# Ten slots for the experts' rows and one kept query block, in place of nine and two

## What is computed

```python
h = rmsnorm(x); proj = h @ w_in        # conv branch, stick-breaking attention, S5 scan
x = x + concat(rmsnorm(parts)) @ w_out
x = x + memory_cross_attention(rmsnorm(x), rmsnorm(mem), w_mq, w_mkv, w_mo)
x = x + peer_ffn(rmsnorm(x), peer_wq, sub_keys, peer_u, peer_v)
```

## Time and profile before

| | |
|---|---|
| median of 3 runs | 1698.66 us (1697.45 to 1699.12) |
| the profiled execution | 1698.56 us, its span in the profile 1696.6 us |
| granted TensorE clock, mean | 0.989 |
| busy share of the span | PE 91%, DVE 69%, ACT 43%, POOL 34% |
| moved by DMA | 675.15 MB, 398 GB/s over the span |
| of it gathers (queue 0) | 536.90 MB |
| of it loads by SP (queue 1) | 137.00 MB |
| first gather issued at | 175.0 us |

### The profile page before, as it was taken

The page is one execution under the profiler, slowest core; times in us unless marked ns, Lnnn a source line. Parts: engine busy times, 40 slices in busy tenths (PEclk is TensorE's granted clock), DMA queues, the critical chain, the costliest instruction groups (busy, mean ns, idle before and its releaser), DMA issues.

```text
span 1696.6 us, 19718 instructions
## 1 busy us (share of the span) xinstructions
PE 1543.3 (91%) x6548; PEld 932.7 (55%) x6548; DVE 1177.5 (69%) x3053; ACT 735.4 (43%) x1971; POOL 577.2 (34%) x527
## 2 busy tenths in 40 slices
PE   9999899899999999888989889988999999777776
PEld 8877776346567776534645446534756554322232
DVE  7821899975877658986555667995656667666654
ACT  4142534763464323385433353465444334333333
POOL 0000344443334323343333343342333544333331
PEclk9999999999999999999999999999999999999999
DMA  9655999999999999999999999999999999999996
GB/s 390 251 199 223 373 416 421 420 421 420 421 420 421 421 419 421 416 417 421 421 421 415 421 414 421 386 422 407 421 412 418 421 421 422 421 421 421 422 420 260
DMA packets 93860, 675.15 MB, mean 398 GB/s; under 512 B 10408, under 2 KB 10688, under 8 KB 12224
## 3 DMA queue, kind: packets, MB, share of 16 engines
q0 software_dynamic: 73728, 536.90, 76.4%
q1 hardware_dynamic: 20032, 137.00, 19.9%
HBM read 672.81 MB, written 1.05 MB: 397 GB/s over the span
## 4 chain that ended last, share of the span: by engine, by line
PE 39%; DMA 32%; DVE 9%; ACT 4%; issue 2%; POOL 0%; DVEq 0%; ACTq 0%; POOLq 0%
DMA slots<-expert_rows,expert 32%; PE bank L967 22%; PE bank L465 8%; DVE slots L1967 5%; PE bank L656 3%; PE bank L952 2%; PE bank L955 2%; ACT diag L1467 1%; ACT coef L1485 1%; DVE sg L1512 1%; PE bank L744 1%; DVE htok L1789 1%; PE bank L723 1%; DVE x L1512 0%; ACT gel L1480 0%
## 5 line engine op out<-in xcount | busy, mean ns | idle before, releaser
L967 PE MATMUL bank<-slots,diag 128*128 128x512 f32 x1916 | 905.6, 609 | 126.8 <-ACT diag L1467 120.4
L1095 POOL DMA_INDIRECT slots<-expert_rows,expert x512 | 575.3, 1124 | 1094.6 <-PE bank L967 880.7
L1967 DVE CUSTOM_DVE_ANT_0 slots<-slots,htok 128x1024 f32<-128x1024 f32 x512 | 626.2, 1224 | 389.6 <-DMA slots<-expert_rows,expert 388.6
L967 PEld LDWEIGHTS bank<-slots,diag 128*128 128x128 f32 x1916 | 348.4, 193 | 537.5 <-issue 317.6
L1480 ACT ACTIVATE gel<-dot 128x2 f32<-128x2 f32 (+1 forms) x258 | 52.5, 204 | 669.2 <-DVE dot L1967 668.3
L465 PEld LDWEIGHTS bank<-hT,ring 128*128 128x128 f32 x1488 | 179.7, 192 | 40.7 <-issue 38.2
L465 PE MATMUL bank<-hT,ring 128*128 128x128 f32 x1488 | 180.7, 276 | 1.8 <-DMA ring<-w_blocks 1.0
L1467 ACT ACTIVATE diag<-ident,coef 128x128 f32<-128x128 f32 x479 | 168.1, 394 | 8.4
L1485 ACT ACTIVATE coef<-gel,gexp 128x1 f32<-128x1 f32 x512 | 123.0, 287 | 10.4
L1480 ACT ACT_TABLE_LOAD x67 | 86.0, 1283 | 1.2
L1512 DVE SCALAR_TENSOR_TENSOR sg<-pad,prm,sg 128x128 f32<-128x128 f32 x240 | 71.8, 345 | 0.0
(11 more groups left out here) (354 smaller groups left out, 1517.7 us busy)
## 6 DMA issues: line engine op xcount, KB each, us to landing
ring<-w_blocks SPq DMA_DIRECT2D x90, 1024.0 KB, 9.1
slots<-w_blocks SPq DMA_DIRECT2D x24, 1024.0 KB, 11.1
slots<-expert_rows,expert POOLq DMA_INDIRECT x512, 16.0
kept<-w_blocks SPq DMA_DIRECT2D x4, 1024.0 KB, 11.9
keys<-w_blocks SPq DMA_DIRECT2D x2, 1024.0 KB, 10.5
kv<-w_blocks SPq DMA_DIRECT2D x2, 1024.0 KB, 13.8
prm<-small SPq DMA_DIRECT2D x2, 768.0 KB, 13.8
x<-x_rows SPq DMA_DIRECT2D x2, 512.0 KB, 11.2
```

The lines of the kernel that those rows point to most:

```text
L967: last = mm(bank[h][:, :], diag[:, i % DIAGS, :], slots[:, SLOT[n], D + h * 512:D + (h + 1) * 512], start=m == 0, stop=n == end)
L1095: nc.gpsimd.indirect_dma_start(slots[:, s, :], None, (experts0_d, experts1_d)[n // PER // NC], bass.IndirectOffsetOnAxis(ap=idx[q % 2][:, ...
L1967: v.tensor_tensor_reduce(out=slots[:, s, 0:D], in0=slots[:, s, 0:D], in1=htok[:, ph % 2, :], scale=1.0, scalar=0.0, op0=ALU.mult, op1=ALU.add,
```

## The change

There is one slot more (slot 9) and one kept place less, so the memory is the same. Layer 0 keeps head 5 alone, layer 1 head 4 alone; so head 4 of layer 0 is loaded again, through the ring, for `ci` 1, and head 3 of layer 1 goes through the ring for `ci` 2 and again for `ci` 3. In `ci` 0 query block 4 is loaded into slot 9 (place `POCKET + 2`) instead of the first kept place. The first 20 gathers take turns over eight slots (0 to 6 and 9), the rest over all ten. Gather 7 is the first in slot 9, and it waits for query block 4.

```diff
--- before.py
+++ after.py
@@ -60,9 +60,9 @@
 
 AHEAD = 1
 
-STAY = 2
+STAY = 1
 POCKET = WIDE + STAY + 2
-SLOTS = 9
+SLOTS = 10
 DIAGS = 4
 WARM = 3
 TP = P + 1
@@ -102,7 +102,7 @@
 
 
 HEADS = [[0, 1, 2, 3, 4, 5], [7, 0, 6, 1, 4, 2, 5, 3], [0, 1, 2, 3, 4], [7, 0, 1, 2, 6, 5, 3, 4]]
-KEPT = [[4, 5], [3, 4]]
+KEPT = [[5], [4]]
 POCKETS = [[6], [6, 5]]
 WQ_AT = [[89, 91, 93, 95, 103, 105], [94 + i * 5 // 2 for i in range(8)],
          [94 + 4 * i for i in range(5)], [94, 98] + [106 + 8 * i for i in range(6)]]
@@ -133,7 +133,7 @@
 
 
 HELD = {2: 8, 3: 7}
-SLOT = [n % 7 for n in range(20)] + [(6, 8, 0, 1, 7, 2, 3, 4, 5)[n % 9] for n in range(NG - 20)]
+SLOT = [(0, 1, 2, 3, 4, 5, 6, 9)[n % 8] for n in range(20)] + [(4, 5, 8, 6, 7, 9, 0, 1, 2, 3)[n % 10] for n in range(NG - 20)]
 
 USED = [SLOT[:n].count(SLOT[n]) for n in range(NG)]
 
@@ -306,7 +306,7 @@
         mats_in = sem("mats_in")
         keys_in = sem("keys_in")
         rows_in = sem("rows_in")
-        loaded = [sem(f"loaded{s}") for s in range(POCKET + 2)]
+        loaded = [sem(f"loaded{s}") for s in range(POCKET + 3)]
         arrived = [sem(f"arrived{s}") for s in range(SLOTS)]
         pair_used = sem("pair_used")
         filled = [sem(f"filled{b}") for b in range(8)]
@@ -384,6 +384,8 @@
                 return POCKET + POCKETS[l].index(h)
             if ci == 1 and what < 2:
                 return WIDE + STAY + what
+            if ci == 0 and h == 4:
+                return POCKET + 2
             if ci == 1 and what in HELD:
                 return place_of_slot(HELD[what])
             r = sum(p < WIDE for p, _ in spots) - sum(l == 0 and c and n in HELD for (l, n), c in zip(order, second))
@@ -412,6 +414,8 @@
                 return (W_, pr_)[p - WIDE - STAY][:, 0:KT * BW]
             if p == POCKET:
                 return kv[:, :]
+            if p == POCKET + 2:
+                return slots[:, 9, :]
             return T[:, :, :, :].rearrange("p t r s -> p (t r s)")[:, 0:KT * BW]
 
         lateT = W_[:, 1024:2048].rearrange("p (t s) -> p t s", t=KT)
@@ -996,9 +1000,9 @@
             nc.sync.dma_start(prm[:, 0:NVEC], prm_d[0, :, 0:NVEC]).then_inc(prm_in, 16)
             nc.sync.dma_start(gains[:, :], rows_d[0, :, :]).then_inc(rows_in, 16)
             stage = 0
-            issue = [j for j in range(len(order)) if spots[j][0] < POCKET]
+            issue = [j for j in range(len(order)) if not POCKET <= spots[j][0] < POCKET + 2]
             for j in range(len(order)):
-                if spots[j][0] >= POCKET:
+                if POCKET <= spots[j][0] < POCKET + 2:
                     l, p = order[j][0], spots[j][0]
                     first = FIRST["mq"] if p == POCKET else FIRST["out"] + 3
                     behind = max(k for k in range(j) if order[k] == (l, first))
@@ -1090,7 +1094,8 @@
                 elif s >= 2:
 
                     done, count = free_at[max(j for j in range(len(order))
-                                              if RING <= spots[j][0] < WIDE and slot_at(spots[j][0]) == s)]
+                                              if RING <= spots[j][0] < WIDE and slot_at(spots[j][0]) == s
+                                              or spots[j][0] == POCKET + 2 and s == 9)]
                     eng.wait_ge(done, count)
                 nc.gpsimd.indirect_dma_start(
                     slots[:, s, :], None, (experts0_d, experts1_d)[n // PER // NC],
```

## The result

The changed kernel takes 1703.82 us (median of 6 runs, 1702.72 to 1707.51), the kernel before 1697.88 us beside it (6 runs, 1696.86 to 1699.12). The difference is 5.94 us, the ratio 1.0037 with an interval of 1.0027 to 1.0047: slower. (The ratios and their intervals are formed from all runs and differ a little from the quotient of the two medians, which is 1.0035 here.) The profiled execution of the changed kernel took 1702.72 us, the quickest of its six, that of before 1698.56 us; two profiles compared with each other therefore show 4.2 us, not 5.9.

A forecast was written before the change was run, and what follows sets the result against it. The slowest DMA engine was taken to bound the kernel. From the profiled 1698.56 us, +4.97 for two loads and +1.1 for the opening gave 1704.63, in terms of the median 1704.7 us; range 1701.2 to 1708.2 us.

The forecast's parts named there:

- The two loads, +4.97: Two more 1 MiB loads, at about 500 and 1370 us, each cost the slowest engine 2.49 us: +4.97 us.
- second rival: The extra loads partly ride along where gathers wait for compute, or one is not made: 1699.8 to 1702 us; chance 8%.
- The tenth slot, 0: One more gather waits in the slowest engine's never-empty queue; dips shrink, the end does not move: 0 us.
- the dips are idle time of the fast engines alone: From 180 to 1680 us, 11 us lost in rate dips are the faster engines' idle time, not the slowest one's.
- first rival: The dips are real and the tenth slot fills them, at most all 11 us: 1693.8 us, faster; chance 8%.
- The queue of the slowest engine is not empty from the first gather to the last.: From 176 us on, the time is the slowest engine's bytes over its rate, plus whatever extra it carries.
- The opening, +1.1: Gather 7 waits for block 4's second half, with 1 us of queued work left: +1.1 us, bounds 0 and +2.8.
- third rival: Gather 7's whole delay of 5.5 us at slot 9 is passed on: 1709.2 us; chance 3%.
- The time of issue: Gather 7, issued at 193.75 us before, would be issued at 199.28 us, behind the second half of block 4.
- The gap in the DMAs: In the opening, a gap of about 1 us in the DMAs near 201 us, as a sign of the forecast.
- SP's order, "I cost this at nothing": Two more issues on SP wait for ring places; what stands behind is the next ring load: cost nothing.
- The forecast of 17.9 us from issue to landing: Gathers late in the span land in about 17.9 us instead of 15.4, with one block more before them.

The follow-up runs named there:

- e5: Kernel before (nine slots) with the two loads more and the memory rows' load put back ahead of the added query block on SP's queue; 1702.87 us, +5.6.
- e12: Changed kernel with gathers 0 to 19 over slots 0 to 6 and the memory rows' load ahead of the added query block; 1703.04 us, +5.5.
- e6: Kernel before with one load, the put-off block into the phasor buffer, made twice from 1101 us on; 1700.74 us, +3.45.
- e2: Kernel before with eight slots in place of nine from gather 20 on; 1700.94 us, +3.6.
- e1: Kernel before with only the two loads more, nine slots and the old rotation; 1705.62 us, +8.3.
- e8: Kernel before, but from gather 200 on three slots keep query blocks of layer 1: three loads less, six slots for gathers; 1747.37 us, +50.
- e4: Changed kernel with gathers 0 to 19 over slots 0 to 6 and slot 9 used from gather 20 on; 1702.67 us, +5.3.
- e3: Changed kernel with the memory rows' load for layer 1 put back ahead of the added query block on SP's queue; 1704.52 us, +7.2.
- e7: Kernel before, but from gather 200 on slot 8 keeps query block 2 of layer 1: one load less, eight slots for gathers; 1695.97 us, -1.3.
- e9: Kernel before with three loads of layer 1's memory keys each cut into 120 and 8 partitions, same bytes; 1712.66 us, +15.5.

## Why the prediction was right, and where its steps were not

The forecast was 1704.7 us, the runs gave 1703.82; its own terms summed to 6.07 us of loss, measured were 5.94. Step by step:

**The two loads, +4.97.** e5 and e12 hold them alone: +5.6 and +5.5. In the profiles 96→160 grew by 2.4 and 2.5 us, 352→384 by 3.2 and 2.3. That also answers the second rival, by which part of the loads rides along. The step is right; whether the half microsecond above 4.97 is real can't be told, since both intervals reach below it (e12's lower end is 0.18%, 3.1 us).

**The tenth slot, 0.** Right as a number, e12 against e5, and right in its reason at the end of the span, where the drip of one engine stands as before. That the dips are idle time of the fast engines alone was read from the trace and not tried: e6, meant to try it, put its load behind the dip. What the traces show for it is that some engine is at work at every moment of the kernel before, and that from gather 96 on the last count of each gather comes 2.5 us or more behind the fifteenth. For the first rival's 1693.8 us nothing is left. The Trainium skill (Perfetto Trace Analysis, Optimization Strategy) says of repeated gaps on the engine that should be saturated that they can mean too few buffers; by that rule the eleven us of dips were the slot's to win. It holds in e2 and in e1, where all engines paused for 1.6 and 1.4 us, and in part in e8. In the kernel before no such pause is found, and there the measurement, e12 against e5, decides against it.

**"The queue of the slowest engine is not empty from the first gather to the last."** No trace names an engine, but the step fits the kernel before and the changed one, and it holds by less than the prediction took it: near gather 22 one slot less empties the queue (e2), and with nine slots the stall of e1 empties it at 522 us. The rows for it were there, 7.5 to 9.6 us at gathers 20 to 23 against 11.6 to 16.9 late in the span.

**The opening, +1.1.** The medians give 0.6 us (the changed kernel against e4) and 1.7 (e3 against e12), 1.1 in the mean of the two pairs; the dot product of gather 20 gives 1.5 between the two kernels with the late opening and the twelve others. The intervals of the medians overlap, so the size is only roughly confirmed. By it the third rival, with 5.5 us, is out. The time of issue was missed by 2 us. POOL's timeline of the changed kernel, gathers 6 to 8, as in the earlier trace rows:

```profile
186.91 1.06 POOL L1100 DMA_INDIRECT slots<-expert_rows,expert  x1 [4.73 <-PE bank L469]
...
197.15 1.05 POOL L1100 DMA_INDIRECT slots<-expert_rows,expert  x1 [9.17 <-PE bank L469]
...
198.50 0.94 POOL L1100 DMA_INDIRECT slots<-expert_rows,expert  x1 [0.30 <-issue]
```

and TensorE's, the two halves of block 4, which stood 3.79 us apart in the earlier trace rows and stand 3.50 apart here:

```profile
191.42 1.95 PE L469 MATMUL bank<-hT,slots 128*128 128x128 f32 x16
193.21 1.88 PE L971 MATMUL bank<-slots,diag 128*128 128x512 f32 x4
194.92 1.95 PE L469 MATMUL bank<-hT,slots 128*128 128x128 f32 x16
```

Gather 7 left at 197.15, not 199.28, because the first half of block 4 already ran at 191.42 instead of 193.27, and not at the lower clock that slowed the work before it (expert 0's four records took 3.43 us from 190.05 in the kernel before, 1.98 us from 189.60 here) and that the windows of 180 to 200 us show for the kernel before:

```profile
180.00:200.00 20.00, 15.70 (x98) 12.26 (x97) 16.10 (x53) 8.85 (x23) 5.77 (x5) 0.91 1.01 415
```

and that those of the changed kernel don't:

```profile
180.00:200.00 20.00, 16.04 (x106) 12.82 (x106) 16.28 (x54) 9.62 (x24) 5.18 (x6) 1.00 0.99 404
```

The granted clock there, 0.91 against 1.00, need not come from the edit: among the twelve kernels with the opening of before it reads 1.00 in three, 0.91 in seven and 0.83 in two. Carrying a single profile's times over to the other kernel was the weak point. The gap in the DMAs came as forecast: from 196 to 208 us the changed kernel moved 4.49 MB and the kernel before 5.04, which is 1.3 us of work. The Trainium skill's figure for a lone transfer (DMA: Bandwidth & Descriptors, Anatomy of one DMA) had made the term 0.9 with the forecast's time of issue. The measured 0.6 to 1.7 us lie on both sides of it and of 1.1, and the time of issue was not the forecast's either, so it decides nothing.

**SP's order, "I cost this at nothing".** This step failed. The prediction said that what stands behind the added load is the next ring load; it is the load of the memory rows, which has 14 us to spare (issued at 466.75, read at 497.9, 17.1 to landing) and was made 21.4 us late. On its own this costs 2.7 us with nine slots (e1 against e5, 2.5 in their profiles) and nothing that the runs can tell with ten: 96→160 takes 222.2 us in the changed kernel and 222.9 in e4 with the stall, 222.0 in e3 and 222.3 in e12 without it. So the tenth slot does earn something in the changed kernel, but only by covering a stall that the change made: it held back up to 2.7 us. The prediction had neither the stall nor a worth for the slot, the two cancel, and in so far the total came out right by luck. A forecast of the loads alone would have been 3.3 us too low (e1: 8.3 against 4.97). The prediction had one sentence near it, that ten slots would hide a TensorE that stands for a late load; it did not look for the load.

**Smaller slips.** The ring has 93 loads, not 92: head 4 of `ci` 1 and head 3 of `ci` 2 and 3 make three more, and the slots take one more while the kept places take two fewer, 120 in all where there were 118. Gather 22 had not waited for the block in slot 7 but gather 24 had, and gather 21 for that in slot 8; it costs nothing either way. The forecast of 17.9 us from issue to landing late in the span could not be read, since some completion counts are missing in the trace of the changed kernel; e7, with one slot less in place of one more, moved as that step says, from 15.4 to 12.6.

**Open.** Which engine is the slow one and what slows it (the code queues' 1.09 MB in the earlier trace rows may be part of it); what a load made inside a dip costs; why packets took longer in e9 and e8; and whether a load costs 2.5 or 2.8 us at the end.

## What to carry to other kernels

A mean rate over 16 DMA engines that dips is no proof that buffers are short: look for the drip of single engines inside the dip, for moments in which no packet at all is under way, and at the time from issue to landing. Here that time was several transfers long, a tenth slot bought nothing that could be measured and each load cost its full time; where it came near the time of a lone transfer, one slot less was dear (2 to 3.6 us for the ninth one, lost just behind the opening), and at six slots the loss was 50 us. And when a load is added to an in-order queue, go through everything behind it until the next slack, loads with conditions of their own above all: here one of them left 21.4 us late. And when an experiment is to put work into a gap, read from its trace when that work really ran: e6's came 6 us behind the gap.

## What was not expected of the hardware

- One gather's 16 completion counts do not come together: in the kernel before the last of the 16 comes 2.5 us behind the fifteenth at gather 100 (485.9 and 488.4 us), 7.7 at gather 200, 5.5 at the last one (1681.1 and 1686.6). It is a single count each time; whether it is always that of the same engine the trace does not say.
- Cutting a load of 128 partitions into 120 and 8 cost some 5 us for each load in a stream that is bound by DMA, with equal bytes and all 16 engines busy: packets of 8 KB took 487 to 539 ns there in place of 312.
- A stall of 8 us on TensorE, with all of a stage's experts behind it, cost 2.7 us with nine slots and nothing that could be measured with ten. With nine all 16 engines paused for 1.4 us of it, with ten none did.
